# Two chained transformer blocks on one core: both blocks in one program section, weight slots and banks shared, with five reorderings

## The chip, the cores and the metric

The kernel runs on one core of a Trainium2 chip. The metric is the device time of one execution in microseconds (us), and the number compared is the median of several runs. TensorE (PE in the profile) multiplies, ScalarE (ACT) and VectorE (DVE) do the element-wise work, GpSimd (POOL) does small square roots and some transfers, and SyncE (SP) issues most transfers from main memory.

## The reference

A batch of one, 256 tokens, width 1024, all in float32. Two models run one after the other, two layers each.

```python
def reference(x, ...):
    x = first_block(x, c, positions, ...)    # per layer: adaLN scale/shift/gate from c, attention with rope and a
                                             # 31-tap conv branch, post-norm; MLP relu(u @ w_up)**2 @ w_down, post-norm:
                                             # x = layer_norm(ALPHA * x + (1 + gt2) * h, ln_ffn_g[l], ln_ffn_b[l])
    return second_block(x, rel_bias_table_2, ...)

def second_block(x, ...):
    for l in range(2):
        h = rmsnorm(x, ln_mix_g[l])
        proj = h @ w_in[l]                   # 1024 x 4128: q, k, v of branches A and B, latents of branch C
        ya = dilated_window_attention(...)   # with a bias looked up from rel_bias_table
        lam = exp(sum(lambda_q1 * lambda_k1)) - exp(sum(lambda_q2 * lambda_k2)) + lam_init
        yb = differential_attention(..., lam, bias_b)
        yc = mla_attention(...)
        x = x + (gates[0] * (ya @ w_br_a) + gates[1] * (yb @ w_br_b) + gates[2] * (yc @ w_br_c)) @ w_o[l]
        h = rmsnorm(x, ln_ffn_g[l])
        x = x + (silu(h @ w_ffn_gate[l]) * (h @ w_ffn_up[l])) @ w_ffn_down[l]
    return rmsnorm(x, final_norm_g)
```

## The kernel before

**Products.** Every large product is float32 split in two parts, a high and a low one. A weight group is 256 rows by up to 512 columns. It passes through a ring of four slots: SP loads it into `w_raw`, ACT rounds it into `w_hi` (line 123), DVE subtracts and leaves `w_lo` (line 129), and TensorE multiplies it with the transposed rows in twelve matmuls (lines 143 to 145: high by high, high by low, low by high, for two chunks and two token halves, tok 0 and 1). SP may load a slot again when its low part is made, and ACT may write `w_hi` again when TensorE has used it. A tile is the four groups that make one bank pair, `prod`; four more banks, `acc`, hold sums, and two, `turn`, take transposes. Rows are transposed on TensorE (line 203), ACT takes the high part (224) and DVE the low part (231).

**Order.** All is written out by hand for each engine, with semaphores between them. Each engine does its instructions in order, and so does SP, whose loads of weights thus stand in one queue with those of vectors.

**The end of a layer of the first block.** Its MLP has eight chunks f = 0 to 7. For each, DVE squares the hidden rows (line 1079), makes four low parts, adds one chunk of the second gate (`gate2_chunk`, line 1059, 128x1024), and makes the low parts of the transposed hidden rows. After the last chunk TensorE sums the gate over the partitions (`sum_rows`, line 1158) and then does the last down product: 48 matmuls into `acc`, tok 0 first. ACT copies the gate out of the bank (629). DVE then adds the residual for each of four half rows (lines 1008, 1012 and 764, `last_residual`), POOL makes the root, and the rows are normed. Between the two layers of the first block the next layer's input is normed first, half by half, with the norm's scale and the modulation folded together in `ada_first` (lines 1112 to 1115), and `x_res` itself (773 and 775, 128x1024) afterwards. At the end of the last layer only `x_res` is made.

**The change of blocks.** The first block ends its program section: all five engines meet at a barrier, and its memory and banks are given back. The second block's section begins with transfers that need its own memory: the flip matrix and the rope table (1539, 1540) and a 1.5 MB transfer from scratch on POOL (1614). TensorE reverses the bias rows with the flip matrix in six banks (12 products of 128x256, line 2199), DVE and ACT copy them out (1526, 1527), and only then does DVE set the semaphores that let SP load the first weights (116) and the norm's vector `mix_g` (1552). After the four groups of the first tile SP issues ten vector transfers (1554 to 1561), the last two being the gate's bias, 1.5 MB, and `ffn_g`, 0.5 MB. The second block's input product has 12 tiles of 344 columns; tiles 0 to 3 hold the latents. DVE waits for all ten vectors, makes the products for lambda (1928 to 1931), and then the low parts of tile 1.

**The end.** After the last down product DVE adds the residual (1861), ACT squares (1673), POOL makes the root (1619 to 1633), DVE multiplies by root and gain at once (1856, 128x1024 for each token half). Another section holds the one transfer of the whole 1 MB output (2438).

## Time and profile before

| what | value |
|---|---|
| median of three runs | 1939.33 us (1937.77 to 1939.8) |
| the profiled execution, its own time | 1941.2 us |
| its span, first to last instruction | 1939.4 us |
| TensorE busy | 1808.5 us, 93% of the span |
| VectorE busy | 1306.2 us, 67% |
| ScalarE busy | 870.9 us, 45% |
| mean granted TensorE clock | 0.976 of full speed |

TensorE is busy nearly all the time, so the table says that time can only be won where TensorE waits or runs at the lower clock. The stretches where it does so are found in the 40 slices of the page, and then in the timeline.

### The profile page before, as it was taken

What the parts mean: (1) busy time and instruction counts of PE and PEld (TensorE: products, weight loads), DVE (VectorE), ACT (ScalarE), POOL (GpSimd) and SP (SyncE); (2) the same over time, 40 slices, a digit from 0 to 9 for tenths busy, and PEclk for the clock granted to TensorE, in tenths of its full rate; (3) what the DMA queues carried; (4) which work ended last, traced back from release to release, by engine and by line L of the source; (5) the groups of instructions that cost most, each with busy time, mean ns of one, the idle gap of its engine ahead of it and who ended that gap; (6) DMA issues with size and microseconds to landing.
All of it is one profiled execution on the core that took longest, in us unless ns stands there. A gap on an engine that the chain in (4) does not pass through costs nothing.

```text
span 1939.4 us, 26122 instructions
## 1 busy us (share of the span) xinstructions
PE 1808.5 (93%) x8358; PEld 1423.0 (73%) x8358; DVE 1306.2 (67%) x2015; ACT 870.9 (45%) x1458; POOL 53.8 (3%) x116
## 2 busy tenths in 40 slices
PE   7989989998989999996699999999999999999997
PEld 3755767886755678884699767788879976778886
DVE  4679886666779886555454788655555478865554
ACT  1434433443334434442355565444445566644443
POOL 0000000000000000000000000000000000000000
PEclk9999999999999999998799999999999999999999
DMA  8755567773755546652566433455565553355653
GB/s 291 250 159 169 182 206 246 243 248 104 260 160 172 174 162 233 202 195 69 187 184 191 147 104 120 152 185 184 178 207 181 178 163 123 102 160 176 195 176 117
DMA packets 210879, 345.90 MB, mean 178 GB/s; under 512 B 20105, under 2 KB 95799, under 8 KB 210533
## 3 DMA queue, kind: packets, MB, share of 16 engines
q1 hardware_dynamic: 208758, 337.79, 53.8%
q0 software_dynamic: 2032, 6.97, 1.1%
q8 instruction: 50, 0.82, 0.2%
q14 instruction: 39, 0.32, 0.1%
HBM read 343.62 MB, written 1.07 MB: 178 GB/s over the span
## 4 chain that ended last, share of the span: by engine, by line
issue 52%; POOLq 1%; POOL 0%; DVE 0%
POOLq L1631 0%; POOLq L1620 0%; POOLq L1629 0%; POOL x_rstd L1632 0%; DVE x_res L1856 0%; POOL gates L1614 0%; POOL x_rstd L1633 0%; POOL sub_rstd L1621 0%; POOL x_squares L1628 0%; POOLq L1639 0%; POOLq L1454 0%; POOL lat_rstd L1621 0%; POOLq L377 0%
## 5 line engine op out<-in xcount | busy, mean ns | idle before, releaser
L129 DVE TENSOR_TENSOR w_lo_b<-w_raw_b,w_hi_b 128x1024 fp32r<-128x1024 f32 (+3 forms) x336 | 362.2, 1100 | 189.5 <-ACT w_hi_b L123 187.9
L123 ACT CAST w_hi_b<-w_raw_b 128x1024 fp32r<-128x1024 f32 (+3 forms) x336 | 313.4, 951 | 167.2 <-PE prod_b L145 79.6
L129 DVE TENSOR_TENSOR w_lo_a<-w_raw_a,w_hi_a 128x1024 fp32r<-128x1024 f32 x232 | 280.6, 1222 | 136.5 <-ACT w_hi_a L123 133.8
L143 PE MATMUL prod_b<-w_hi_b,hT_hi 128*128 128x512 f32 (+1 forms) x912 | 342.7, 376 | 14.3 <-ACT proj_b L1661 8.2
L123 ACT CAST w_hi_a<-w_raw_a 128x1024 fp32r<-128x1024 f32 x232 | 240.9, 1049 | 234.2 <-PE acc_a L145 115.1
L145 PE MATMUL prod_b<-w_hi_b,hT_lo 128*128 128x512 f32 (+1 forms) x912 | 334.6, 367 | 0.0
L144 PE MATMUL prod_b<-w_lo_b,hT_hi 128*128 128x512 f32 (+1 forms) x912 | 333.5, 366 | 0.0
L143 PE MATMUL prod_a<-w_hi_a,uT_hi 128*128 128x512 f32 x592 | 244.8, 413 | 18.3 <-DVE w_lo_a L129 9.4
L145 PE MATMUL prod_a<-w_hi_a,uT_lo 128*128 128x512 f32 x592 | 237.6, 401 | 0.0
L144 PE MATMUL prod_a<-w_lo_a,uT_hi 128*128 128x512 f32 x592 | 237.5, 401 | 0.0
L143 PEld LDWEIGHTS prod_b<-w_hi_b,hT_hi 128*128 128x128 f32 x912 | 173.1, 190 | 45.7 <-DVE w_lo_b L129 13.0
L145 PEld LDWEIGHTS prod_b<-w_hi_b,hT_lo 128*128 128x128 f32 x912 | 173.1, 190 | 24.1
L144 PEld LDWEIGHTS prod_b<-w_lo_b,hT_hi 128*128 128x128 f32 x912 | 173.5, 190 | 21.1
L143 PEld LDWEIGHTS prod_a<-w_hi_a,uT_hi 128*128 128x128 f32 x592 | 113.4, 191 | 57.9 <-issue 17.2
L145 PEld LDWEIGHTS prod_a<-w_hi_a,uT_lo 128*128 128x128 f32 x592 | 113.4, 192 | 27.9
L144 PEld LDWEIGHTS prod_a<-w_lo_a,uT_hi 128*128 128x128 f32 x592 | 113.7, 192 | 24.4
L143 PE MATMUL acc_a<-w_hi_a,aT_hi 128*128 128x512 f32 x272 | 111.8, 411 | 4.5 <-DVE w_lo_a L129 4.5
L916 DVE SCALAR_TENSOR_TENSOR conv_acc<-hpad,conv_wT,conv_acc 128x256 f32<-128x256 f32 x232 | 102.5, 482 | 10.5 <-issue 1.3
L144 PE MATMUL acc_a<-w_lo_a,aT_hi 128*128 128x512 f32 x272 | 109.3, 402 | 0.0
L145 PE MATMUL acc_a<-w_hi_a,aT_lo 128*128 128x512 f32 x272 | 108.8, 400 | 0.0
L143 PEld LDWEIGHTS acc_a<-w_hi_a,aT_hi 128*128 128x128 f32 x272 | 52.3, 192 | 18.7 <-issue 6.2
L1232 PE MATMUL acc_a<-ada_raw,c_wide 128*128 128x512 f32 x128 | 62.4, 633 | 0.0
(320 smaller groups left out, 2446.5 us busy)
## 6 DMA issues: line engine op xcount, KB each, us to landing
w_raw_a<-in_w_in_dram SPq DMA_DIRECT2D x72, 512.0 KB, 4.2
w_raw_b<-in_w_in_dram SPq DMA_DIRECT2D x192, 172.0 KB, 2.4
w_raw_a<-in_w_up_dram SPq DMA_DIRECT2D x64, 512.0 KB, 4.7
w_raw_a<-in_w_down_dram SPq DMA_DIRECT2D x64, 512.0 KB, 4.5
ada_raw<-in_w_ada_dram SPq DMA_DIRECT2D x52, 512.0 KB, 6.6
w_raw_b<-in_w_gate_dram SPq DMA_DIRECT2D x96, 256.0 KB, 3.1
w_raw_b<-in_w_ffn_gate_dram SPq DMA_DIRECT2D x88, 256.0 KB, 3.5
w_raw_b<-in_w_ffn_up_dram SPq DMA_DIRECT2D x88, 256.0 KB, 4.2
```

Source lines behind the costliest of these rows:

```text
L123: act.copy(self.hi[:, s, 0:cols], self.raw[:, s, 0:cols]).then_inc(self.hi_done, 1)
L129: dve.tensor_tensor(self.lo[:, s, 0:cols], self.raw[:, s, 0:cols], self.hi[:, s, 0:cols].bitcast(F32), ALU.subtract).then_inc(self.lo_done, 1)
L143: pe.matmul(out, a_hi, w_hi, start=first and c == 0, stop=False)
L144: pe.matmul(out, a_hi, w_lo, start=False, stop=False)
L145: mm = pe.matmul(out, a_lo, w_hi, start=False, stop=last and c == chunks - 1)
L916: dve.scalar_tensor_tensor(out, rows, w, out, ALU.mult, ALU.add)
L1232: mm = pe.matmul(acc[0][:, :], c_wide[:, 2 * i + k, :], ada_raw[:, i, k * NT:(k + 1) * NT], start=i + k == 0, stop=False)
```

## The change

1. Both blocks are written into one section: `first_block` and `second_block` return one function for each engine, which run one after the other. The weight ring, its semaphores, `prod`, `acc`, `turn` and their semaphores are made once; the second block counts on from `GROUPS1`, `TILES1`, `TURNS1` and `SPLITS1`.
2. The second block's first eight weight groups are loaded right behind the first block's last. `mix_g` is loaded in the middle of the first block's last layer. The second block's first input is normed straight from the first block's statistics (`first_h`, with `ada_first` = the last norm's vectors times `mix_g`), low parts of weights between, and `x_res` itself (`last_x`) after it.
3. What needs the first block's memory to be free (flip, rope table, six small vectors, the 1.5 MB bias transfer) waits on `first_left`, which DVE sets behind `last_x`. Tiles 1, 2 and 3 go to the `acc` pairs and back to `prod`; the bias rows are reversed behind tile 3 (four banks) and tile 4 (two banks).
4. The gate's bias and `ffn_g` are loaded behind all groups of `w_in`, in both layers of the second block.
5. The low parts of tiles 1 to 3 come before the lambda products, in both layers.
6. The gate chunk of f = 7 comes before its four low parts, in both layers of the first block.
7. At the end root and gain are split: DVE multiplies by the gain early, POOL does fewer steps, DVE scales the left half rows and ACT the right, and four transfers of 256 KB leave from SP and ACT.

```diff
@@ class Weights @@
-        sp.wait_ge(self.lo_done, pos.count(1))
+        sp.wait_ge(self.lo_done, pos.count(1 + self.groups))
@@ first_block, sync, last layer's MLP @@
+                else:
+                    sp.dma_start(mix_g[:, :], dr["ln_mix_g_2"][0:1, :].to_broadcast([P, D])).then_inc(mix_in, 16)
@@ first_block, vector, hidden() @@
+                    if f == T_FF - 1:
+                        gate2_chunk(f)
                     if after:
                         split(after)
...
-                    gate2_chunk(f)
+                    if f < T_FF - 1:
+                        gate2_chunk(f)
@@ first_block, vector, end @@
+                else:
+                    dve.wait_ge(mix_in, 16)
+                    for v in range(2):
+                        dve.tensor_tensor(ada_first[:, v, :], ln_vec[:, 1 - v, :], mix_g[:, :], ALU.mult)
+                    dve.drain()
...
+            def first_h(tok, h):
+                cols = slice(h * NT, (h + 1) * NT)
+                if h == 0:
+                    dve.wait_ge(ln_rstd, layer(LAYERS - 1, TOKS + tok, 2 * TOKS).count(1))
+                normed(u_rows[:, tok, cols], x_res[:, tok, cols], tok, ada_first[:, 1, cols], ada_first[:, 0, cols]).then_inc(u_ready, 1)
@@ second_block, sync @@
-            sp.dma_start(flip, dr["flip"]).then_inc(consts_in, 16)
-            sp.dma_start(trig[:, :, :], dr["trig_2"].rearrange("(t p) e -> p t e", p=P)).then_inc(consts_in, 16)
...
-                in_tile(IN2_T - LAT_TILES, layer(l, 0, G2))
+                for t in range(2):
+                    in_tile(IN2_T - LAT_TILES + t, layer(l, 4 * t, G2))
+                if l == 0:
+                    sp.wait_ge(first_left, 1)
+                    sp.dma_start(flip, dr["flip"]).then_inc(consts_in, 16)
+                    sp.dma_start(trig[:, :, :], dr["trig_2"].rearrange("(t p) e -> p t e", p=P)).then_inc(consts_in, 16)
...
-                sp.dma_start(gates[:, 0, :], row("b_gate", 3 * D)).then_inc(vec_in, 16)
-                sp.dma_start(ffn_g[:, :], row("ln_ffn_g", D)).then_inc(vec_in, 16)
-                with sp.Fori(1, LAT_TILES) as t:
+                with sp.Fori(2, LAT_TILES) as t:
                     in_tile(t + (IN2_T - LAT_TILES), Pos(0, (l, G2), (t, 4)))
                 with sp.Fori(0, IN2_T - LAT_TILES) as t:
                     in_tile(t, Pos(4 * LAT_TILES, (l, G2), (t, 4)))
+                sp.dma_start(gates[:, 0, :], row("b_gate", 3 * D)).then_inc(late_in, 16)
+                sp.dma_start(ffn_g[:, :], row("ln_ffn_g", D)).then_inc(late_in, 16)
@@ second_block, scalar @@
+                if l == 0:
+                    split(layer(l, 0, G2), 4, KG * IN2_W)
+                    for n in range(4):
+                        take_h_hi(n)
+                    split(layer(l, 4, G2), 4, KG * IN2_W)
...
                 for tok in range(TOKS):
                     square_x(2 * l, tok)
+                if l == 0:
+                    split(layer(l, 8, G2), 4, KG * IN2_W)
@@ second_block, vector @@
+                if l == 0:
+                    last_residual(0, 0)
+                    last_residual(0, 1)
+                    split(layer(l, 0, G2), 1, KG * IN2_W)
+                    last_residual(1, 0)
+                    first_h(0, 0)
+                    first_h(0, 1)
+                    take_h_lo(0)
+                    last_residual(1, 1)
+                    split(layer(l, 1, G2), 2, KG * IN2_W)
...
+                    for tok in range(TOKS):
+                        split(layer(l, 4 + 2 * tok, G2), 2, KG * IN2_W)
+                        last_x(tok).then_inc(x_halves, 2)
+                    dve.drain().then_inc(first_left, 1)
@@ second_block, the end @@
+            for tok in range(TOKS):
+                act.wait_ge(x_gained, 2 * tok + 2)
+                act.wait_ge(x_rstd_done, 2 * TOKS * LAYERS + tok + 1)
+                act.activation(x_res[:, tok, NT:D], h_rows[:, tok, NT:D], ACT.Copy, scale=x_rstd[:, 0, tok:tok + 1])\
+                   .then_inc(scaled, 1)
+                act.wait_ge(scaled, tok + 1)
+                act.dma_start(out[0, tok * P:(tok + 1) * P, NT:D], x_res[:, tok, NT:D]).then_inc(out_done, 16)
```

Three places show how the rows move. The first is DVE's order at the last MLP chunk of the first block's second layer (names as in the code; `w_lo` is the low part of a weight group). Before:

```order
L1079 TENSOR_TENSOR proj<-proj 128x512 [waits prod_free0_a]
L1079 TENSOR_TENSOR proj<-proj 128x512 [waits prod_free1_a]
L129 TENSOR_TENSOR w_lo_a<-w_raw_a,w_hi_a 128x1024 [waits w_hi_done_a] x4
L1059 SCALAR_TENSOR_TENSOR proj<-proj,c_act 128x1024 [waits gate2_in1]
L231 SCALAR_TENSOR_TENSOR aT_lo<-turn_a,aT_hi 128x4x128 [waits turn_hi_a] x2
L1008 SCALAR_TENSOR_TENSOR proj<-ada_rest,acc_a 128x512 [waits down0_done,ada_taken,vec_in]
```

And in the changed kernel:

```order
L1080 TENSOR_TENSOR proj<-proj 128x512 [waits prod_free0]
L1080 TENSOR_TENSOR proj<-proj 128x512 [waits prod_free1]
L1060 SCALAR_TENSOR_TENSOR proj<-proj,c_act 128x1024 [waits gate2_in1]
L134 TENSOR_TENSOR w_lo<-w_raw,w_hi 128x1024 [waits w_hi_done] x4
L241 SCALAR_TENSOR_TENSOR aT_lo<-turn,aT_hi 128x4x128 [waits turn_hi] x2
L1124 TENSOR_TENSOR ada_first<-ln_vec,mix_g 128x1024 [waits mix_g_in,vec_in]
L1124 TENSOR_TENSOR ada_first<-ln_vec,mix_g 128x1024
L1009 SCALAR_TENSOR_TENSOR proj<-ada_rest,acc 128x512 [waits ada_taken,down0_done,mix_g_in]
```

The gate chunk has moved ahead of the four low parts, and two multiplications by `mix_g` stand ahead of the first residual.

The second is SP's queue around the change of blocks. Before:

```order
L116 DMA w_raw_a<-in_w_down_dram 128x2x512 [waits w_lo_done_a] x8
L1531 UNCONDITIONAL_BRANCH [waits barrier_Pool_Activation_PE_DVE_SP_release]
L1539 DMA proj_b<-in_flip_dram 128x128
L1540 DMA trig_b<-in_trig_dram 128x2x32
L1552 DMA mix_g<-in_ln_mix_g_dram 128x1024 [waits vec_free]
L116 DMA w_raw_b<-in_w_in_dram 128x344 [waits w_lo_done_b]
L116 DMA w_raw_b<-in_w_in_dram 128x344
...
L1554 DMA lat_g<-in_mla_q_norm_g_dram 128x768
...
L1560 DMA gates<-in_b_gate_dram 128x3072
L1561 DMA ffn_g<-in_ln_ffn_g_dram 128x1024
```

And in the changed kernel, where eight loads of `w_in`, not four, stand ahead of the wait:

```order
L121 DMA w_raw<-in_w_down_dram 128x2x512 [waits w_lo_done] x8
L121 DMA w_raw<-in_w_in_dram 128x344 [waits w_lo_done]
L121 DMA w_raw<-in_w_in_dram 128x344
...
L1573 DMA proj_b<-in_flip_dram 128x128 [waits first_left]
L1574 DMA trig_b<-in_trig_dram 128x2x32
L1575 DMA lat_g<-in_mla_q_norm_g_dram 128x768
L1576 DMA lat_g<-in_mla_kv_norm_g_dram 128x256
L1578 DMA lam_vec<-in_lambda_q_2_dram 128x64 x2
L1578 DMA lam_vec<-in_lambda_k_2_dram 128x64 x2
L1579 DMA lam_const<-in_lam_const_dram 128x2
L1580 DMA sub_g<-in_diff_subln_g_dram 128x128
```

The barrier and the wait for the bias are gone from ahead of the weights. Tile 2's weights (the ninth group and on) now stand behind `first_left` and the eight small transfers, and `b_gate` and `ffn_g` have gone down the queue, to just ahead of the first group of `w_uq`.

The third is TensorE's order at the same change. Before:

```order
L2157 UNCONDITIONAL_BRANCH [waits barrier_Pool_Activation_PE_DVE_SP_release]
L2199 MATMUL prod_b<-gates,proj_b 128x256 [waits bias_in,consts_in_b]
L2199 MATMUL prod_b<-gates,proj_b 128x256 x3
L2199 MATMUL acc_b<-gates,proj_b 128x256 x8
L203 MATMUL turn_b<-ident,proj_b 128x128 [waits turn_free0_b,h_ready_b]
```

In the changed kernel the reversal comes behind tile 3 and tile 4 (between the two pieces stand the 48 matmuls of tile 4):

```order
L2286 MATMUL acc<-gates,proj_b 128x256 [waits prod_free0,prod_free1,bias_in,consts_in_b]
L2286 MATMUL acc<-gates,proj_b 128x256 x7
L148 MATMUL prod<-w_hi,hT_hi 128x344 [waits w_lo_done,prod_free0]
...
L2286 MATMUL acc<-gates,proj_b 128x256 [waits bias_out]
L2286 MATMUL acc<-gates,proj_b 128x256
```

Four tiles of the second block thus run before TensorE needs anything that was loaded after the first block had left its memory, except tile 2's and 3's weights.

## Rows read from the trace of the kernel before

**Rows 1.** The page's 40 slices: TensorE's granted clock, in tenths of full speed.

```profile
PEclk9999999999999999998799999999999999999999
```

**Rows 2.** A stretch: busy us (records) by engine, then clock, DMA share, GB/s.

```profile
910.00:930.00 20.00, 6.35 (x23) 5.40 (x24) 6.61 (x9) 1.72 (x4) 3.17 (x3) 0.58 0.27 84
```

**Rows 3.** TensorE's timeline, change of blocks: start, us, op, tiles, idle before and releaser.

```profile
891.88 3.15 PE L1158 MATMUL prod_a<-proj,ones 128*128 128x512 f32 x4 [3.06 <-DVE proj L1059]
894.04 1.42 PE L143 MATMUL acc_a<-w_hi_a,aT_hi 128*128 128x512 f32 x1
...
906.36 0.40 PE L145 MATMUL acc_a<-w_hi_a,aT_lo 128*128 128x512 f32 x1
923.65 3.46 PE L2199 MATMUL prod_b<-gates,proj_b 128*128 128x256 f32 x8 [16.90 <-DMA gates<-bias_rows_dram]
926.95 3.62 PE L2199 MATMUL acc_b<-gates,proj_b 128*128 128x256 f32 x16
...
940.38 0.63 PE L143 MATMUL prod_b<-w_hi_b,hT_hi 128*128 128x344 f32 x1 [1.43 <-DVE w_lo_b L129]
...
957.08 0.65 PE L143 MATMUL prod_b<-w_hi_b,hT_hi 128*128 128x344 f32 x1 [6.45 <-ACT proj_b L1661]
...
989.58 0.35 PE L143 MATMUL prod_b<-w_hi_b,hT_hi 128*128 128x344 f32 x1
```

**Rows 4.** DVE's timeline at the first block's last gate chunk.

```profile
890.54 1.28 DVE L1059 SCALAR_TENSOR_TENSOR proj<-proj,c_act 128x1024 f32<-128x1024 f32 x1
891.74 1.28 DVE L231 SCALAR_TENSOR_TENSOR aT_lo<-turn_a,aT_hi 128x512 fp32r<-128x512 f32 x2
```

**Rows 5.** TensorE's timeline between the first block's two layers.

```profile
455.49 1.88 PE L1158 MATMUL prod_a<-ada_first,ones 128*128 128x512 f32 x4
...
461.93 3.28 PE L1158 MATMUL prod_a<-proj,ones 128*128 128x512 f32 x4 [3.69 <-DVE proj L1059]
464.23 1.41 PE L143 MATMUL acc_a<-w_hi_a,aT_hi 128*128 128x512 f32 x1
...
480.88 0.76 PE L143 MATMUL prod_a<-w_hi_a,uT_hi 128*128 128x512 f32 x1 [1.52 <-issue]
```

**Rows 6.** DVE's timeline: `x_res` normed between the layers, and later three low parts.

```profile
493.79 1.29 DVE L773 SCALAR_TENSOR_TENSOR x_res<-x_res,mv,ln_vec 128x1024 f32<-128x1024 f32 x1
...
954.71 2.71 DVE L129 TENSOR_TENSOR w_lo_b<-w_raw_b,w_hi_b 128x688 fp32r<-128x688 f32 x3 [0.97 <-ACT w_hi_b L123]
```

**Rows 7.** The page's transfers: issuer, count, KB each, median us to landing.

```profile
w_raw_b<-in_w_in_dram SPq DMA_DIRECT2D x192, 172.0 KB, 2.4
...
gates<-in_b_gate_dram SPq DMA_DIRECT2D x2, 1536.0 KB, 9.2
...
ffn_g<-in_ln_ffn_g_dram SPq DMA_DIRECT2D x2, 512.0 KB, 11.1
out_dram<-x_res SPq DMA_DIRECT2D x1, 1024.0 KB, 4.0
...
sub_g<-in_diff_subln_g_dram SPq DMA_DIRECT2D x2, 64.0 KB, 6.5
```

**Rows 8.** Transfers issued from 942 to 943 us (behind `b_gate` and `ffn_g`).

```profile
w_raw_b<-in_w_in_dram SPq DMA_DIRECT2D x1, 172.0 KB, 9.7
```

**Rows 9.** SP's queue: one vector's issue, and the first group of `w_uq`.

```profile
940.43 0.43 SPq L1559 DMA_DIRECT2D sub_g<-in_diff_subln_g_dram  x1
...
1031.91 11.35 SPq L116 DMA_DIRECT2D w_raw_b<-in_w_uq_dram  x12
```

**Rows 10.** ACT's and TensorE's timelines at that group: its rounding, its first matmul.

```profile
1038.70 0.84 ACT L123 CAST w_hi_b<-w_raw_b 128x768 fp32r<-128x768 f32 x1 [0.54 <-PE prod_b L145]
...
1045.07 0.42 PE L143 MATMUL prod_b<-w_hi_b,yaT_hi 128*128 128x384 f32 x1
```

**Rows 11.** DVE's and SP's timelines at the end of the program.

```profile
1933.45 1.28 DVE L1856 SCALAR_TENSOR_TENSOR x_res<-x_res,x_rstd,mix_g 128x1024 f32<-128x1024 f32 x1 [1.59 <-POOL x_rstd L1633]
...
1934.99 0.40 SPq L2438 DMA_DIRECT2D out_dram<-x_res  x1
```

395 lines of the change are left out of this document (237 added, 158 removed).

## The prediction

> **What bounds the kernel now.** I read the page first. TensorE is busy for 1808.5 of 1939.4 us, so an edit is worth what it takes out of TensorE's waits or out of its time at the lower clock. The 40 slices of the granted clock are full except at the 19th and 20th [rows 1], the change from the first block to the second. So I read that stretch in windows: from 910 to 930 us TensorE is busy for 6.35 of 20 us at a granted clock of 0.58, and the transfer engines have a share of 0.27 [rows 2]. Nothing is the bound there; it is a chain of waits. TensorE's timeline gives it link by link [rows 3]: the first block's last matmul starts at 906.36 and ends at 906.76; TensorE then waits 16.90 us for the bias transfer and reverses the bias until 930.6; the first matmul of tile 0 comes at 940.38, because the weights and `mix_g` are asked for only then; tile 1 comes at 957.08 after another 6.45 us, behind the ten vector transfers. Tile 5, from which both kernels do the same work in the same order, starts at 989.58. That start is my marker.
>
> The same view shows a smaller wait at the end of each layer of the first block: TensorE idles 3.06 us [rows 3] and 3.69 us [rows 5] for the gate chunk, and the matmul that follows the sum takes 1.42 and 1.41 us where later ones take 0.40 [rows 3, 5]: the clock has dropped to its lower level, 1.2 GHz.
>
> **The gate chunk first (two layers).** DVE makes the chunk at 890.54, right behind its four low parts, and the low parts of the hidden rows at 891.74, until 893.02 [rows 4]. With the chunk moved ahead, 1.20 us leave this place: the hidden low parts are done at 891.8. The gate sum no longer waits; unthrottled it takes 1.88 us [rows 5], and started 3.06 us earlier, at 888.8, it is over at 890.7. So the low parts are the next to be late, and the down product starts at about 892.0 instead of 894.04 [rows 3]: 2.0 us. The moved chunk delays one low part of weights by 1.2 us; what hides that is the ring of four groups ahead of TensorE, whose 48 matmuls take 12.7 us (894.04 to 906.76 [rows 3]). The idle time falls from 3.06 to some 1.3 us, which may or may not keep the clock up. The 1.42 us matmul and the slow ones behind it are worth up to 1.3 us; I take 0.8, for between 0 and 1.3. So **2.8 us** in each layer, bounds 2.0 and 3.3. The first layer's is a term of its own; the second's goes into the next.
>
> **The change of blocks.** The model for the new sequence is in the trace: between the first block's two layers DVE does the same residuals, norm and low parts in the same order. There the down product starts at 464.23 and the next layer's first matmul at 480.88 [rows 5]: 16.65 us, less the same 0.8 of clock, 15.9. From 892.0 that puts tile 0 at 907.9 instead of 940.38. The two extra multiplications by `mix_g`, 128x1024 like those of 1.28 us [rows 4], take 2.6 us and lie beside the first quarter of the down product, some 3 of its 12.7 us; without that cover they would cost 2.6.
>
> From the first matmul at 480.88 to DVE's first instruction on `x_res` at 493.79 are 12.9 us [rows 5, 6], which ends the low parts of the input: 920.8. Now DVE makes four low parts of tile 1, of 0.9 us [rows 6], and norms `x_res`, four instructions of 1.29 us [rows 6]: 8.7 us. `first_left` comes at 929.5. TensorE runs out of work at the same time: tile 1 starts near 921 and takes about 8.
>
> Then SP stands where it stood not before: it issues ten small transfers ahead of tile 2's weights, 0.43 us each and a gap [rows 9], 4.5 in all, so these are issued at 934.0. When they land is not shown. Such a load takes 2.4 us in an undisturbed queue [rows 7] and 9.7 behind all ten vectors of before [rows 8]. Of those, 2 MB are gone from ahead of it, but the bias transfer of 1.5 MB on POOL starts at the same time, and the small vectors are slow themselves (`sub_g`, 64 KB, takes 6.5 [rows 7]). I take 6.0, nearer to the middle, which gives 940.0. Rounding and low part, 0.8 and 0.9 us, bring TensorE to 941.7: **a new wait of 12 us**, with the lower clock behind it.
>
> Tiles 1 to 4 took from 957.08 to 989.58, 32.5 us, with the same slow start [rows 3]. Three tiles take 24.8 (three quarters, and the whole of the slow start). The reversal is the same work, 16 records in 3.62 us at full clock [rows 3], so 5.4 for 24. Its inputs have long landed by 958, and its copies lie beside tile 4. Tile 5 starts at 941.7 + 24.8 + 5.4 = 971.9, against 989.58: **17.7 us** earlier. Bounds from the landing: 2.4 gives 21.3; 9.7 gives 14.0.
>
> In the second block's second layer the lambda products waited for nothing that TensorE missed, so their move is worth nothing there; in the first layer it is in the sum above.
>
> **The late vectors (two layers).** `b_gate` and `ffn_g` now stand ahead of the first group of `w_uq`, which was issued at 1031.91 [rows 9], rounded at 1038.70 and multiplied at 1045.07 [rows 10]. So there are 13.2 us from issue to use. `ffn_g` lands 11.1 us after its issue [rows 7], and the group behind it some 1 us later, near 1044; rounding, the latents' high and low parts that ACT and DVE do behind it, and the low part take 2 to 4 us. That is 1 to 3 us late, with a slow start up to 5. But the 11.1 was measured with six vectors ahead; alone, the two may land in 8, which hides them. Bounds 0 and 5 us for each layer; I take 1, nearer to the hidden end: **+2.0 us**.
>
> **The end.** The last multiplication waits 1.59 us for POOL, takes 1.28 us and ends at 1934.73; the transfer is issued at 1934.99 and lands 4.0 us later [rows 7, 11]. POOL has two steps to do instead of five behind the last square: about 0.9 of the 1.59. A half row takes half of 1.28: 0.6. The last pair is 512 KB instead of 1 MB; between 2.4 us for 172 KB and 4.0 for 1 MB [rows 7] I take 3.4: 0.6. Together **2.1 us**, bounds 0.9 and 3.5. The Trainium skill, "DMA: Bandwidth & Descriptors", section "Rules for kernel authors", speaks against the four transfers: transfers of two halves serialize, and queues of several engines share the same 16 transfer engines, so the split adds no bandwidth. By that rule the term loses its last 0.6 and the time is 0.6 us longer; no row here has a store of half the size to decide it.
>
> **Sum.** 2.8 + 17.7 − 2.0 + 2.1 = 20.6 us off a span of 1939.4: 1918.8. The profiled execution's own time (1941.2) lies 1.8 above its span, and the median (1939.33) is where the span is; I apply the difference to the median: **1918.7 us**.
>
> **Rivals.**
> (a) *Tile 2's weights come much later.* For it: the 9.7 us row [rows 8], and POOL's 1.5 MB at the same time. 9.7 us and 3 more for sharing put tile 5 at 978.6; the time is 1925.4. Against it: the 2 MB ahead are gone. The same page of the Trainium skill, section "Queues, rings and completion order", says that a transfer engine goes round between the queues that have work, packet by packet; by that rule POOL's transfer and SP's share from 930 on, as in this rival. Chance 0.2; it lies in my range.
> (b) *The late vectors are exposed*, 4 to 5 us in each layer: 1925 to 1929 with the rest as forecast, up to 1935 together with (a). For it: 11.1 us. Against it: 13.2 us of room. Chance beyond the range 0.1.
> (c) *No change:* what comes off at the change of blocks comes back at the first group of `w_uq`. It needs 10 to 13 us in each layer. 1936 to 1943, 0.04.
> (d) *Slower:* the late vectors hold up not one group of `w_uq` but all six, since each load waits for a low part that waits for the one before, and TensorE restarts slowly twice: 11.1 us and 4 more in each layer, 30 in all, against 22.6 gained: 1946.8. It decides from 11.3 us a layer. The 13.2 us of room speak against it. 0.04.
> (e) *More gain:* weights at 2.4 us, clock kept, vectors hidden: 3.6 + 1 + 2 + 1.4 less, 1911; beyond 1909, 0.06.
>
> **How the numbers follow.** The forecast, with (a), (b) and (e) as far as they stay between 1909 and 1929, has 0.76. From 1929 to 1935 there are 0.1. A measurement of this kernel tells 0.2%, 3.9 us, from no change. Faster is 0.76 + 0.1 + 0.06, or 0.92; same 0.04; slower 0.04.
>
> **What would show it.** The gate sum ahead of the last down product without a wait, and that product's first matmul under 1.4 us. Tile 0 at about 905 (908 less the first layer's 2.8). A wait of about 12 us ahead of tile 2, ended by ACT's rounding, which waited for `w_raw`. The reversal behind tile 3 with no wait of its own. At the first group of `w_uq` a TensorE wait of 0 to 3 us. I am wrong if tile 2's wait is under 8 or over 16 us, or if ACT waits for `w_uq` for more than 5 us.

## The result, and the profile after

The changed kernel takes **1921.3 us** (median of four runs, 1917.55 to 1923.12), beside 1939.57 us for the kernel before on the same chip: a ratio of 0.9903, 95% interval 0.9891 to 0.9915. The forecast was 1918.7, range 1909 to 1929. The profiled execution has a span of 1921.2 us, 18.2 less than before.

The page of the changed kernel, its line of the granted clock. The low slices, 8 and 7 in [rows 1], are 8 and 8.

```profile
PEclk9999999999999999998899999999999999999999
```

TensorE's timeline of the changed kernel, both ends of the first block's layers and the change of blocks (start, us, op, tiles, idle before and releaser); it answers to [rows 3, 5].

```profile
454.83 1.88 PE L1170 MATMUL prod<-ada_first,ones 128*128 128x512 f32 x4
...
461.33 0.47 PE L148 MATMUL acc<-w_hi,aT_hi 128*128 128x512 f32 x1 [1.40 <-DVE aT_lo L241]
...
476.86 0.77 PE L148 MATMUL prod<-w_hi,uT_hi 128*128 128x512 f32 x1 [1.52 <-issue]
...
884.42 1.88 PE L1170 MATMUL prod<-proj,ones 128*128 128x512 f32 x4
887.69 0.47 PE L148 MATMUL acc<-w_hi,aT_hi 128*128 128x512 f32 x1 [1.40 <-DVE aT_lo L241]
...
898.77 0.40 PE L150 MATMUL acc<-w_hi,aT_lo 128*128 128x512 f32 x1
900.51 0.65 PE L213 MATMUL turn<-ident,proj 128*128 128x128 f32 x4 [1.34 <-DVE proj L776]
902.64 0.63 PE L148 MATMUL prod<-w_hi,hT_hi 128*128 128x344 f32 x1 [1.48 <-issue]
...
940.66 0.65 PE L148 MATMUL acc<-w_hi,hT_hi 128*128 128x344 f32 x1 [15.20 <-DVE w_lo L134]
...
958.44 3.61 PE L2286 MATMUL acc<-gates,proj_b 128*128 128x256 f32 x16
...
971.00 0.51 PE L148 MATMUL prod<-w_hi,hT_hi 128*128 128x344 f32 x1
...
1028.19 0.42 PE L148 MATMUL prod<-w_hi,yaT_hi 128*128 128x384 f32 x1 [1.45 <-DVE ybT_lo L241]
```

The gate sum of the second layer has no wait and the down product behind it starts at a short 0.47 us. Tile 0 of the second block starts at 902.64 instead of 940.38, 3.5 us behind the first block's last matmul. Then stands the new wait, 15.20 us ahead of tile 2, and the marker, tile 5, at 971.00 instead of 989.58. The wait is opened in the queues of SP, POOL and ACT.

```profile
924.42 0.33 SPq L1573 DMA_DIRECT2D proj_b<-in_flip_dram  x1
...
929.57 0.44 SPq L1580 DMA_DIRECT2D sub_g<-in_diff_subln_g_dram  x1
930.37 82.60 SPq L121 DMA_DIRECT2D w_raw<-in_w_in_dram  x80
```

```profile
924.69 1.09 POOL L1639 DMA_DIRECT2D gates<-bias_rows_dram  x1 [17.45 <-DVEq L1984]
925.80 0.20 POOL L1653 TENSOR_TENSOR x_squares<-x_sq 128x1 f32<-128x1 f32 x1
935.56 0.19 POOL L1644 TENSOR_TENSOR x_squares<-x_squares,small 128x1 f32<-128x1 f32 x1 [9.56 <-issue]
```

```profile
938.93 1.62 ACT L128 CAST w_hi<-w_raw 128x688 fp32r<-128x688 f32 x2 [13.22 <-DMA w_raw<-in_w_in_dram]
```

`first_left` comes at 924.4, the ten small transfers (flip, rope table and the eight of the vectors) take 5.95 us of SP, tile 2's first group is issued at 930.37 and rounded at 938.93, 8.56 us later. Of POOL's root one instruction runs behind the transfer and the next starts 9.56 us later; the last section shows what it waits for.

At the end (ACT's timeline, and the view of the transfers: count, KB each, median us to landing), for [rows 7, 11]:

```profile
1917.53 0.72 ACT L1902 ACTIVATE x_res<-proj_b,x_rstd 128x512 f32<-128x512 f32 x1 [0.64 <-POOL x_rstd L1676]
1918.28 0.34 ACTq L1905 DMA_DIRECT2D out_dram<-x_res  x1
```

```profile
out_dram<-x_res SPq DMA_DIRECT2D x2, 256.0 KB, 2.1
out_dram<-x_res ACTq DMA_DIRECT2D x2, 256.0 KB, 2.6
```

The start of TensorE's last matmul, the mark for the end's term, in the kernel before and in the changed one:

```profile
1929.25 0.40 PE L145 MATMUL acc_b<-w_hi_b,yaT_lo 128*128 128x512 f32 x1
```

```profile
1914.36 0.40 PE L150 MATMUL acc<-w_hi,yaT_lo 128*128 128x512 f32 x1
```

**The ledger** is the difference of start times between the two traces at the same work. Before anything that differs it is −0.66 already (454.83 for 455.49), scatter between two executions. At the second layer's first matmul it is −4.02, at tile 5 −18.58, at the first group of `w_uq` −16.88 (1028.19 for 1045.07), at the last matmul of the program −14.89 (1914.36 for 1929.25), at the end of the span −18.2. The loss of 2.0 us between `w_uq` and the last matmul belongs to this one trace: the second trace of the changed kernel (e11) gains 1.0 there (1029.06 and 1912.22 at the same two places).

### The profile page after: what moved, and what is told of

Read it like the earlier page. It is cut to its first block, busy times and chain, and to the rows that moved or that the text cites. A ratio compares the mean times of both kernels' runs of the same rounds, so it can differ in the third digit from the quotient of the medians.

```text
span 1921.2 us, 26005 instructions
## 1 busy us (share of the span) xinstructions
PE 1807.1 (94%) x8358; PEld 1423.2 (74%) x8358; DVE 1310.8 (68%) x2025; ACT 871.5 (45%) x1460; POOL 53.0 (3%) x112
## 4 chain that ended last, share of the span: by engine, by line
issue 52%; PE 30%; DVE 10%; DVEq 4%; ACT 1%; POOLq 1%; DMA 1%; SPq 1%; POOL 0%; ACTq 0%
PE prod L148 5%; PE prod L150 5%; PE prod L149 5%; PE acc L148 4%; PE acc L150 4%; PE acc L149 4%; DVE w_lo L134 3%; DVE conv_acc L917 2%; DVEq L916 2%; PE acc L1244 2%; PE turn L213 1%; DMA ada_rest<-in_w_ada_dram 1%; DVEq L775 1%; DVE stats L765 0%; DVE x_res L1013 0%
## 5 line engine op out<-in xcount | busy, mean ns | idle before, releaser
L134 DVE TENSOR_TENSOR w_lo<-w_raw,w_hi 128x1024 fp32r<-128x1024 f32 (+3 forms) x568 | 642.1, 1150 | 339.1 <-ACT w_hi L128 334.5
L128 ACT CAST w_hi<-w_raw 128x1024 fp32r<-128x1024 f32 (+3 forms) x568 | 554.2, 990 | 416.4 <-PE acc L150 197.0
L148 PE MATMUL prod<-w_hi,hT_hi 128*128 128x512 f32 (+1 forms) x880 | 332.2, 378 | 8.2 <-ACT kv_up L1687 1.8
L150 PE MATMUL prod<-w_hi,hT_lo 128*128 128x512 f32 (+1 forms) x880 | 323.9, 368 | 0.0
L149 PE MATMUL prod<-w_lo,hT_hi 128*128 128x512 f32 (+1 forms) x880 | 322.8, 367 | 0.0
L148 PE MATMUL prod<-w_hi,uT_hi 128*128 128x512 f32 x592 | 244.7, 413 | 17.1 <-DVE w_lo L134 8.0
L150 PE MATMUL prod<-w_hi,uT_lo 128*128 128x512 f32 x592 | 237.9, 402 | 0.0
L149 PE MATMUL prod<-w_lo,uT_hi 128*128 128x512 f32 x592 | 237.7, 402 | 0.0
L150 PEld LDWEIGHTS prod<-w_hi,hT_lo 128*128 128x128 f32 x880 | 166.6, 189 | 24.0
L149 PEld LDWEIGHTS prod<-w_lo,hT_hi 128*128 128x128 f32 x880 | 167.1, 190 | 21.2
L148 PE MATMUL acc<-w_hi,hT_hi 128*128 128x512 f32 (+1 forms) x144 | 57.2, 397 | 19.8 <-DVE w_lo L134 17.7
L149 PEld LDWEIGHTS acc<-w_lo,aT_hi 128*128 128x128 f32 x272 | 51.9, 191 | 12.7 <-issue 0.2
```

Of the source, the lines that this page charges most:

```text
L128: act.copy(self.hi[:, s, 0:cols], self.raw[:, s, 0:cols]).then_inc(self.hi_done, 1)
L134: dve.tensor_tensor(self.lo[:, s, 0:cols], self.raw[:, s, 0:cols], self.hi[:, s, 0:cols].bitcast(F32), ALU.subtract).then_inc(self.lo_done, 1)
L148: pe.matmul(out, a_hi, w_hi, start=first and c == 0, stop=False)
L149: pe.matmul(out, a_hi, w_lo, start=False, stop=False)
L150: mm = pe.matmul(out, a_lo, w_hi, start=False, stop=last and c == chunks - 1)
```

## The experiments

All times are medians; each run was timed beside the kernel before on the same chip. "The changed kernel" is 1921.3, and 1921.0 in a second run of it (e11).

**e1, the gate chunk back behind its low parts.**

```diff
-                    if f == T_FF - 1:
-                        gate2_chunk(f)
                     if after:
                         split(after)
...
-                    if f < T_FF - 1:
-                        gate2_chunk(f)
+                    gate2_chunk(f)
```

> The changed kernel with its sixth part undone: the gate chunk of f = 7 stands again behind its four low parts, in both layers of the first block. Theory T (the chunk's place is worth its start and the clock behind it): each layer loses 2.2 us of start of the last down product and 1.1 to 1.2 us of clock in that product, 3.4 us a layer as between the two traces, and nothing hides it, because the second layer's loss also moves first_left and so tile 2's weights: 1928.1 us, +6.8 on 1921.3, ratio to the kernel before 0.994. The first matmul of the down product takes 1.4 us again. Rival R1 (the second layer's part is covered by the wait of 15.20 us ahead of tile 2): 1924.7, +3.4. Rival R2 (only the clock is won, the start comes from elsewhere in the merged section): +2.4, 1923.7.

Measured: 1926.04 us, ratio 0.9930 (0.9916 to 0.9943): 4.7 to 5.0 us slower than the changed kernel, between T and R1. The trace shows T's two pieces, and something given back behind them that T missed. TensorE's timeline of e1:

```profile
480.95 0.77 PE L148 MATMUL prod<-w_hi,uT_hi 128*128 128x512 f32 x1 [1.52 <-issue]
...
910.32 0.63 PE L148 MATMUL prod<-w_hi,hT_hi 128*128 128x344 f32 x1 [1.48 <-issue]
...
947.14 0.65 PE L148 MATMUL acc<-w_hi,hT_hi 128*128 128x344 f32 x1 [15.11 <-DVE w_lo L134]
```

The first layer ends 4.1 us later and tile 0 starts 7.7 us later than in the changed kernel, of which 0.75 is scatter that stands ahead of anything that differs (455.58 for 454.83). So the two layers lose 3.3 and 3.6 us, as T said. But tile 2 starts only 6.5 us later. The difference is the clock in tile 0. In windows of 10 us from the start of tile 0 (busy us and records by engine, then granted clock, DMA share, GB/s), first of e1, then of the changed kernel:

```profile
910.32:920.32 10.00, 8.52 (x39) 6.72 (x40) 8.51 (x13) 1.20 (x2) 1.70 (x2) 0.86 0.36 108
```

```profile
902.64:912.64 10.00, 9.46 (x34) 8.74 (x35) 7.63 (x12) 1.20 (x2) 1.71 (x2) 0.52 0.35 108
```

So R1's reason, the wait ahead of tile 2 as a cover, is refuted: the wait is as long as ever (15.11 us), and the missing 1.2 us are tile 0's clock: `first_left` comes 20.65 us behind tile 0 here, and 21.8 in the changed kernel. Another 0.9 come back between tile 2 and the reversal, which take 16.84 us at a granted clock of 0.89 for 17.78 at 0.84. That leaves 4.8 at tile 5 (5.54 less the 0.75), the measured cost. Whether the chunk's place has a part in that clock stays open: it was 0.52 to 0.54 in eight traces with the chunk early, but 0.86 in e5's and full in e4's and e8's.

**e12, the same part alone in the kernel before** (the edit of e1 reversed, in the kernel before).

> The kernel before with the sixth part alone: the gate chunk of f = 7 ahead of its four low parts. It prices that part without the changed change of blocks. Theory T: 3.4 us in each layer (start 2.2, clock 1.1 to 1.2), and the second layer's is not hidden, because the barrier and everything behind it follow the last matmul: 1932.5 to 1933.5, -6.8 us. Rival R (as undoing it in the changed kernel cost only 4.7 to 5.2, a part is given back behind it in either kernel): -4.5 to -5.5 us, 1934 to 1935.

Measured: 1933.92 us, ratio 0.9968 (0.9956 to 0.9980): 6.0 us faster, and by the ratio 6.2, between 3.9 and 8.5. T (6.8) fits, R (5.5 at most) is not excluded. The trace has both: up to the reversal it is 6.6 us ahead of the kernel before (915.24 for 923.65, less 1.8 of scatter at the start), and then the reversal runs at a granted clock of 0.65 instead of 0.78 and tile 0 is only 4.7 ahead. Together with e1 the part is worth 5 to 6 us.

**e2, tile 2's loads ahead of `first_left`.**

```diff
-                for t in range(2):
+                for t in range(3 if l == 0 else 2):
                     in_tile(IN2_T - LAT_TILES + t, layer(l, 4 * t, G2))
...
-                with sp.Fori(2, LAT_TILES) as t:
+                with sp.Fori(3 if l == 0 else 2, LAT_TILES) as t:
```

> The four loads of tile 2's weights are issued ahead of the wait for first_left and the ten small transfers; all else as in the changed kernel. Theory T (the 15.20 us wait is SP's place in the queue: 1.6 us until first_left, 6.0 for the ten issues, 8.5 to landing): loads issued by 921.7, rounding by ACT right behind its squares at 925.8, tile 2 at 927.5 instead of 940.66. Tile 3's weights then stand behind the small transfers, and its bank pair behind the root that POOL finishes at 938.4: tile 3 at about 941 to 943 instead of 950.87, a wait of 3 to 6 us ahead of it, total 1912 to 1914, -8 us. Rival R1 (the wait only moves: tile 3 now waits for the landing as tile 2 did and the time stays within 2 us): 1919 to 1922. Rival R2 (the bias transfer comes late behind it and the reversal waits): tile 3 as in T but a wait ahead of the reversal, 1916 or more.

Measured: 1913.74 us, ratio 0.9869 (0.9854 to 0.9884), 7.4 us faster than the changed kernel, as T said. Its TensorE and ACT timelines:

```profile
926.72 0.43 PE L148 MATMUL acc<-w_hi,hT_hi 128*128 128x344 f32 x1 [1.87 <-DVE w_lo L134]
...
941.02 0.63 PE L148 MATMUL prod<-w_hi,hT_hi 128*128 128x344 f32 x1 [6.46 <-DVE w_lo L134]
```

```profile
938.33 0.99 ACT L1693 ACTIVATE proj_b<-prod,x_rstd 128x344 f32<-128x344 f32 x2 [10.57 <-POOL x_rstd L1658]
939.20 1.44 ACT L128 CAST w_hi<-w_raw 128x688 fp32r<-128x688 f32 x2
```

The wait of 15.20 us is now 1.87, and 6.46 us stand ahead of tile 3. Two things end within 1 us of each other there. ACT waits 10.57 us for POOL's root, and tile 3's rounding stands behind it in ACT's order. But tile 3's first group, issued behind the ten small transfers and beside POOL's transfer, has landed whole only at 938.99, 0.2 us ahead of its rounding, so its landing alone would have cost almost as much.

**e3, tile 2's loads behind `first_left` but ahead of the ten small transfers.**

```diff
                     sp.wait_ge(first_left, 1)
+                    in_tile(IN2_T - LAT_TILES + 2, layer(l, 8, G2))
                     sp.dma_start(flip, dr["flip"]).then_inc(consts_in, 16)
```

> Tile 2's four loads stay behind the wait for first_left but go ahead of the ten small transfers. It tells the landing from the issue. Theory T (ten issues cost 6.0 us, and the vectors' own packets most of the 8.5 us landing, since they stand ahead in the same queue): first load issued at 924.4, landed by 928 although POOL's 1.5 MB start at the same time, tile 2 at 930 instead of 940.66; tile 3 again waits for weights behind the vectors, at 943 to 945 instead of 950.87: 1914 to 1916, -6 us. Rival R1 (the bias transfer is what makes the landing slow): landing stays at 8 us, first load landed at 932.5, tile 2 at 934.3 and tile 3 at 946 to 950: 1917 to 1920, -1 to -4 us.

Measured: 1914.51 us, ratio 0.9865 (0.9850 to 0.9881), T's time, for half of T's reason. ACT's timeline of e3:

```profile
927.70 0.76 ACT L128 CAST w_hi<-w_raw 128x688 fp32r<-128x688 f32 x1 [1.62 <-DMA w_raw<-in_w_in_dram]
934.74 0.76 ACT L128 CAST w_hi<-w_raw 128x688 fp32r<-128x688 f32 x1 [6.28 <-DMA w_raw<-in_w_in_dram]
```

The view of the transfers of e3, issues from 924 to 925 us, and then from 926 to 927:

```profile
w_raw<-in_w_in_dram SPq DMA_DIRECT2D x1, 172.0 KB, 2.4
...
w_raw<-in_w_in_dram SPq DMA_DIRECT2D x3, 172.0 KB, 7.9
```

TensorE starts tile 2 at 929.43 and waits once more, 3.36 us, at 936.47. Only what is issued at once lands as fast as T wanted. What is issued from 926 on, beside POOL's 1.5 MB and ahead of all vectors, lands 7.9 us after its issue, as R1 said. The Trainium skill, "DMA: Bandwidth & Descriptors", section "Queues, rings and completion order", says that a transfer engine goes round between the queues that have work, a packet at a time; these rows agree, since nothing but weights stood ahead in SP's queue.

**e4, the bias transfer later** (POOL: roots first, then a wait for the twelfth rounded group, then the transfer).

```diff
+                if l == 0:
+                    pool.wait_ge(first_left, 1)
+                    pool.wait_ge(bias_rows.in_dram, 16)
+                    pool.wait_ge(W.hi_done, layer(0, 11, G2).count(1 + W.groups))
+                    pool.dma_start(bias_flipped, bass.AP(tensor=scratch.tensor, offset=0,
+                                                         ap=[[1, P], [REL, AH + BH], [1, SEQ]])).then_inc(bias_in, 16)
```

> POOL issues the bias transfer behind its first roots and only once the sixteenth-less-four, that is the twelfth, weight group is rounded, so it shares nothing with tile 2's weights; the ten small transfers stay ahead. Theory T (sharing: 1.5 MB of the 3 MB moved between 925 and 937 us are the bias, at some 300 GB/s 4 to 5 us): tile 2's first group lands 4 to 5 us after its issue instead of 8.5, tile 2 at 936.5 instead of 940.66, the bias lands by 951 ahead of its reversal: 1917 to 1918, -4 us. The roots, which POOL made only at 935.6 to 938.4, are made by 929. Rival R1 (the small vectors' many packets make the landing slow, the bias none of it): landing stays 8 us, 1921, no change. Rival R2 (the bias is late for its reversal): a wait of some us ahead of the reversal, 1921 or more.

Measured: 1916.66 us, ratio 0.9883 (0.9867 to 0.9899), 4.4 to 4.6 us faster, T's time. SP's, ACT's and TensorE's timelines of e4:

```profile
928.52 30.01 SPq L121 DMA_DIRECT2D w_raw<-in_w_in_dram  x32
```

```profile
934.86 1.63 ACT L128 CAST w_hi<-w_raw 128x688 fp32r<-128x688 f32 x2 [10.04 <-DMA w_raw<-in_w_in_dram]
```

```profile
936.59 0.66 PE L148 MATMUL acc<-w_hi,hT_hi 128*128 128x344 f32 x1 [12.00 <-DVE w_lo L134]
```

Without POOL's transfer beside them the ten issues take 4.99 us (923.53 to 928.52) instead of 5.95, and issue to rounding is 6.34 us instead of 8.56. Those are 3.2 us, all of the step from a wait of 15.20 to one of 12.00. In this run tile 0 also ran at full clock, which chance gave (last section): `first_left` comes 20.6 us behind tile 0 instead of 21.8. So 1.1 of the 4.1 us by which tile 2 starts earlier in this trace are not the edit's, and T's 936.5 was met partly by luck; the landing, 5.2 and 5.8 us for the two loads of the first group, was slower than T's 4 to 5.

**e5, both causes together, and tile 3's loads ahead of the eight vectors** (edits of e2 and e4; the transfer waits for the thirteenth group).

> Both causes of the wait ahead of tile 2 and of the one that e2 moved to tile 3 are taken away together: tile 2's loads ahead of first_left as in e2, tile 3's loads behind flip and rope table but ahead of the eight vectors, POOL's roots ahead of its bias transfer, and that transfer issued only when tile 3's first group is rounded. Theory T (SP's place in the queue and POOL's transfer are all that TensorE waits for here): tile 2 at 926.7 as in e2, tile 3 at 934 to 936 with a wait under 2 us, the reversal near 943, tile 5 at 955 to 957 instead of 971.00 (e2: 963.18): 1905 to 1908, -14 us on the changed kernel and -7 on e2. Rival R1 (the bias transfer, issued near 931 and landing 11 us later, is late for its reversal): a wait of 2 to 5 us ahead of the reversal, 1909 to 1911. Rival R2 (the vectors, now ahead of tile 4's weights and beside the bias transfer, make tile 4 wait as they did tile 3): 4 to 6 us back, 1911 to 1913.

Measured: 1910.13 us, ratio 0.9844 (0.9831 to 0.9858); T's 1905 to 1908 is missed. Both rivals' waits are there, each smaller than they said: 1.35 us ahead of the reversal, 2.13 ahead of tile 4. ACT's and TensorE's timelines of e5:

```profile
946.07 1.67 ACT L128 CAST w_hi<-w_raw 128x688 fp32r<-128x688 f32 x2 [7.89 <-DMA w_raw<-in_w_in_dram]
```

```profile
944.01 3.69 PE L2289 MATMUL acc<-gates,proj_b 128*128 128x256 f32 x16 [1.35 <-issue]
949.83 0.43 PE L148 MATMUL prod<-w_hi,hT_hi 128*128 128x344 f32 x1 [2.13 <-ACT proj_b L1696]
```

**e9, the eight vectors behind tile 4's loads, the bias transfer right behind the roots** (tile 2's loads ahead of `first_left`, as in e2).

```diff
                     sp.dma_start(trig[:, :, :], dr["trig_2"].rearrange("(t p) e -> p t e", p=P)).then_inc(consts_in, 16)
+                    in_tile(IN2_T - LAT_TILES + 3, layer(l, 12, G2))
+                    in_tile(0, layer(l, 16, G2))
```

> e5 gave 1910.1 with two small waits left: 1.35 us ahead of the reversal (bias issued 931.36, landed 12.6 later) and 2.13 us and a slow start ahead of tile 4, whose weights were issued at 937.55 behind the vectors and landed near 946. Here the eight vectors go behind tile 4's loads as well, and POOL issues the bias transfer right behind its roots, near 929, without waiting for a rounded group. Theory T (both waits come from these two places): no wait ahead of the reversal, tile 4 directly behind it at 946 to 947 instead of 949.83, tile 5 at 956 to 957 instead of 960.59: 1906 to 1907. Rival R1 (the bias transfer now shares with tile 3's weights and gives the time back ahead of tile 3): a wait of 2 us or more there, 1909 to 1911. Rival R2 (the vectors behind tile 4 delay tile 5's weights): the wait moves on to tile 5, 1909 or more.

Measured: 1905.74 us, ratio 0.9831 (0.9818 to 0.9845): T. TensorE's timeline of e9:

```profile
926.25 0.43 PE L148 MATMUL acc<-w_hi,hT_hi 128*128 128x344 f32 x1 [1.87 <-DVE w_lo L134]
...
938.84 0.43 PE L148 MATMUL prod<-w_hi,hT_hi 128*128 128x344 f32 x1 [0.96 <-DVE w_lo L134]
...
942.74 3.61 PE L2289 MATMUL acc<-gates,proj_b 128*128 128x256 f32 x16
```

Waits of 1.87 and 0.96 us are left of 15.20, and the reversal has none. R1's sharing is there in small: of tile 3's loads those issued up to 928.0 landed in 2.3 to 4.2 us, and the one issued at 928.50, behind POOL's transfer (927.76), in 8.6.

**e6, the late vectors in four pieces of 512 KB, one behind each of the last four tiles of `w_in`, in both layers.**

```diff
-                sp.dma_start(gates[:, 0, :], row("b_gate", 3 * D)).then_inc(late_in, 16)
-                sp.dma_start(ffn_g[:, :], row("ln_ffn_g", D)).then_inc(late_in, 16)
+                for t in range(4, IN2_T - LAT_TILES):
+                    in_tile(t, layer(l, 4 * LAT_TILES + 4 * t, G2))
+                    if t < 7:
+                        cols = slice((t - 4) * D, (t - 3) * D)
+                        sp.dma_start(gates[:, 0, cols], dr["b_gate_2"][ls, cols].to_broadcast([P, D])).then_inc(late_in, 16)
+                    else:
+                        sp.dma_start(ffn_g[:, :], row("ln_ffn_g", D)).then_inc(late_in, 16)
```

> The changed kernel with b_gate in three transfers of 512 KB and ffn_g as a fourth, one behind each of the last four tiles of w_in, in both layers, instead of 2 MB in one go ahead of w_uq. Theory T (the late vectors cost 1.5 to 2.5 us a layer at the first groups of w_uq, as the waits of 1.45 and 1.97 us and the shifts between the two traces say): those waits are gone, 1917 to 1919, -2 to -4 us. Rival R1 (the shift in the second layer is scatter from run to run, and the first's is all): -1.5 us, 1919.8. Rival R2 (the pieces hold up w_in's own groups): new waits in w_in's last tiles, 1921 or more.

Measured: 1918.35 us, ratio 0.9886 (0.9871 to 0.9901), 2.7 to 3.0 us faster, as T said; the interval doesn't exclude R1's 1919.8. The traces say that both layers have a part, the second a small one: from tile 5 to the last matmul e6 takes 938.2 us and e11, the changed kernel again, 940.3. From tile 5 to the first group of `w_uq` there are 57.19 us in the changed kernel (57.12 in e7 and e11), 55.64 in e6, and 55.49 before. The first matmuls of that group in e6's two layers have no wait, where the ten traces of the changed kernel and its variants with the vectors in one go have 0.56 to 1.97 us in the second layer:

```profile
1028.00 0.42 PE L148 MATMUL prod<-w_hi,yaT_hi 128*128 128x384 f32 x1
...
1519.90 0.42 PE L148 MATMUL prod<-w_hi,yaT_hi 128*128 128x384 f32 x1
```

**e7, one store of 1 MB from SP.**

```diff
+            sp.wait_ge(out_ready, TOKS)
+            sp.wait_ge(scaled, TOKS)
+            sp.dma_start(out.rearrange("a (t p) d -> p (a t) d", p=P), x_res[:, :, :]).then_inc(out_done, 16)
```

> The changed kernel, with one transfer of 1 MB from SP when all four half rows are scaled, instead of four of 256 KB from SP and ACT. It measures the last part of the end's term. Theory T (the rest of the end's gain is not in the stores): the last scaling ends where it did, 18.25 - 14.36 = 3.9 us behind TensorE's last matmul's start, and the store takes 4.0 us and 0.3 to issue instead of 2.6: the stretch from the last matmul's start to the end is 8.4 us instead of 6.84 and the time 1.6 us longer, 1922.9. Rival R1 (by the Trainium skill, DMA: Bandwidth & Descriptors, Rules for kernel authors, a split adds no bandwidth): the store costs the same either way and the stretch stays within 0.3 us of 6.84, 1921.3.

Measured: 1922.68 us, ratio 0.9915 (0.9901 to 0.9928); the interval alone doesn't decide, the trace does. ACT's last scaling, SP's store and its landing in e7:

```profile
1913.80 0.72 ACT L1902 ACTIVATE x_res<-proj_b,x_rstd 128x512 f32<-128x512 f32 x1 [0.64 <-POOL x_rstd L1676]
```

```profile
1914.60 0.40 SPq L1632 DMA_DIRECT2D out_dram<-x_res  x1
```

```profile
out_dram<-x_res SPq DMA_DIRECT2D x1, 1024.0 KB, 4.1
```

From the last matmul's start (1910.63) to the end of the span (1919.0) are 8.37 us, T's 8.4, against 6.84 (1914.36 to 1921.2) with four stores. The split is worth 1.5 us. The rule of the Trainium skill ("DMA: Bandwidth & Descriptors", section "Rules for kernel authors") that splitting adds no bandwidth is not contradicted: three quarters of the output leave before the last half row is scaled, and what remains on the path is a store of 256 KB that lands 2.6 us after its issue.

**e8, the lambda products ahead of the low parts again** (DVE's wait for the vectors and its four instructions stand ahead of the loop over the low parts).

> The changed kernel with its fifth part undone: DVE waits for the vectors and makes the lambda products ahead of the low parts of tile 2 and on in the first layer of the second block (of tile 1 and on in the second), not behind those of tile 4. Theory T (worth nothing where the weights land behind the vectors anyway): in the first layer four small instructions, 1 us at most, stand between the weights' landing and tile 2's low parts, and may lie inside the wait; in the second layer 0. 1921 to 1922.5. Rival R1 (the wait on the vectors was a part of the 6.45 us that the kernel before lost ahead of its tile 1): 3 us or more ahead of tile 2, 1924 or more.

Measured: 1927.75 us, ratio 0.9938 (0.9925 to 0.9952), 6.5 to 6.7 us slower. Neither theory: in the first layer it costs next to nothing (tile 2's wait is 15.54 us), in the second, where T said 0, all. DVE's and TensorE's timelines there, and the same matmul in the changed kernel:

```profile
1433.85 0.29 DVE L2000 TENSOR_TENSOR lam_prod<-lam_vec 128x128 f32<-128x128 f32 x1 [7.82 <-DMA sub_g<-in_diff_subln_g_dram]
```

```profile
1435.56 0.65 PE L148 MATMUL prod<-w_hi,hT_hi 128*128 128x344 f32 x1 [5.06 <-DVE w_lo L134]
```

```profile
1433.56 0.42 PE L148 MATMUL prod<-w_hi,hT_hi 128*128 128x344 f32 x1 [1.70 <-ACT proj_b L1693]
```

The wait ahead of tile 1 is 3.4 us longer than in the changed kernel, and the granted clock over the 10 us behind it is 0.77 instead of 1.00. The cause is the second part of the change: it loads tile 1's weights ahead of the vectors in the second layer too (`for t in range(2)` in the diff), and those loads wait for free slots. So the last small vector lands 14.6 us behind tile 0's first matmul here, where in the kernel before even `ffn_g`, the last of ten, landed 6.0 us behind it. The fifth part is what keeps DVE from waiting for them.

**e10, everything moved** (e9 and e6 together).

> e9 and e6 together: vectors behind tile 4, bias right behind the roots, b_gate and ffn_g in four pieces in w_in's last tiles. Theory T (the two gains lie in different places of the program and add): e9's time less 2.5 to 3 us, 1903 to 1904.5, ratio to the kernel before 0.981. Rival R (with the change of blocks shorter, SP's queue is fuller at w_in's last tiles and the pieces hold it up): e9's time less 1 us at most.

Measured: 1904.57 us, ratio 0.9816 (0.9803 to 0.9829), the best of all: some 35 us faster than the kernel before and 16.5 faster than the changed one. On e9 it gains 1.2 us by the medians, 2.9 by the ratios; the intervals overlap. The traces say more: from tile 5 to the last matmul e10 takes 938.3 us and e9 941.8, so the pieces gain 3.5 us there, as T said, and no wait is left at `w_uq`. But tile 5 itself starts at 957.66 instead of 955.30, behind waits of 1.48 us ahead of tile 3 and 0.90 ahead of tile 5. Those lie ahead of the first piece, in the part that is the same as e9's, so they are no sign of R; e9's trace has 0.96 and none.

**e11, the changed kernel again.**

> The changed kernel once more, unedited, to see what repeats of its trace. Expected: a median of 1920 to 1922.5. The wait ahead of tile 2 within 0.4 us of 15.2, as in e1, e6, e7 and e8 (15.1 to 15.5). At the first groups of w_uq in the second layer the stretch from its tile 1 to the first matmul with the latents' second half was 107.8 us in the changed kernel's first trace and 105.3 to 105.8 in e1, e2, e3, e5 and e7, which are the same there: if the 107.8 was scatter it is 105 to 106 here, if not it is 107.8 again.

Measured: 1921.02 us, ratio 0.9897 (0.9881 to 0.9912). The wait ahead of tile 2 is 15.12 us: it repeats. The second layer's stretch at `w_uq` does not. The windows from its first `w_uq` matmul to the first on the second half of the latents, first of the changed kernel's first trace, then of e11:

```profile
1522.18:1541.39 19.21, 17.54 (x89) 16.61 (x89) 8.36 (x11) 9.96 (x18) 0.00 (x0) 0.91 0.60 177
```

```profile
1521.56:1539.21 17.65, 15.97 (x88) 15.06 (x89) 8.36 (x11) 9.97 (x18) 0.00 (x0) 1.00 0.63 196
```

The wait ahead of it was 1.97 us in the first and 0.56 in e11, and the clock fell in the first alone (0.91 for 1.00): 1.56 us of the ledger are scatter, and 1.5 more between the two layers' `w_uq` groups. Counted from the first mark (455.49), e11 ends 21.0 us ahead of the kernel before, and the changed kernel's first trace 17.5; the medians of the two are only 0.3 us apart.

## Why the prediction was right, and by how much each step was off

**The gate chunk.** Forecast 2.8 us a layer. The first layer gives 4.02 − 0.66 = 3.4: the start 2.24 earlier (461.33 for 464.23, less the 0.66), the clock 1.12 (16.65 us from that matmul to the next layer's first became 15.53). The second layer's product starts at 887.69, or 891.7 on the time axis of the kernel before, forecast 892.0. Both layers together were forecast at 5.6 us; the ledger says 6.5 to 7, the medians of e1 and e12 say 5 to 6.

**Tile 0.** Forecast 907.9 without the first layer's shift, measured 902.64 + 4.02 = 906.7 on the same axis. The stretch between the layers was the right model; the chain was 14.95 us instead of 15.9.

**The wait ahead of tile 2.** Forecast 12 us, measured 15.20, within the 8 to 16 that I had set. It ended as said: DVE's low part came right behind ACT's rounding, which had waited 13.22 us for `w_raw`. `first_left` was right (21.8 us behind tile 0, 21.6 forecast), and so was rounding and low part (1.73 for 1.7). Two terms were mis-sized: the ten issues took 5.95 for 4.5 us, and issue to rounding, which I had marked as not shown, 8.56 for 6.0, together 4.0 too little. Tile 2 came 38.0 us behind tile 0 instead of 33.8. The wait grew less than that, because tiles 0 and 1 kept TensorE for 22.8 us and not 21.6, at the lower clock. e4 shows 3.2 of it to be POOL's transfer, 1.0 in the issues and 2.2 in the landing. Rival (a) named the sharing with POOL's transfer and sized it too high (12.7 for 8.56).

**Tile 2 to tile 5.** 30.3 us, forecast 30.2; the reversal had no wait, as said.

**The sum of the change of blocks.** 18.58 − 4.02 = 14.6 us, forecast 17.7, bounds 14.0 to 21.3. No run takes the first three parts of the change back one by one: that the 14.6 come from the barrier, the bias and the loads that no longer stand ahead of tile 0 is read from the two traces.

**The late vectors.** Forecast 1 us a layer. The first layer lost 1.7 (57.19 for 55.49 us), e6 gave back 1.55 of it, and in all 2.7 to 3.0 us for two layers by the medians: right mechanism, up to 1 us too little. ACT waited 4.2 and 4.6 us for `w_uq`, under the 5 that I had set. In the second layer the cost scatters (waits of 0.56 to 1.97 us in repeated traces).

**The lambda products.** "Worth nothing there", said of the second layer, failed. I compared with the kernel before, where the vectors stood ahead of tile 1's weights, and did not ask what the part is worth beside the second one. e8: without it 6.5 us are lost. The forecast of the whole was not hurt, since both parts are in the kernel; that was luck.

**The end.** Forecast 2.1 us, measured 10.15 − 6.84 = 3.3, near the upper bound of 3.5. e7 shows the store to be 1.5 of it, where I had 0.6 for a smaller last pair.

In sum the forecast took 20.6 us off the span and 18.2 came off. Short of the forecast are 3.1 at the change of blocks, 0.7 at the first layer's late vectors and 1.0 behind them (the ledger goes from −16.88 to −14.89, forecast 1 us; e11 shows this last one to be scatter); beyond it are 0.6 in the first layer, 1.2 at the end and 0.66 of scatter at the start. So 4.8 us of one sign stand against 2.5 of the other: the mechanisms were right, and that the total was nearer than its parts is partly luck. Two traces of the same kernel differ by 3.5 us in this ledger, so a difference of 1 us in a single entry behind tile 5 tells nothing.

## What to carry to other kernels

When a barrier between two stages is taken away, the next limit is the first transfer that still waits for memory to be given back: put every load that doesn't need that memory ahead of the wait in its queue (e2, 7.4 us), and the vectors that are read late behind the weights that are read next (with that and the later bias transfer, e9, 15.4 us, beside the 18.3 of the change itself). Issue a large transfer on an engine only behind that engine's own short work that others wait for, above all where a drain stands in that work (next section). A large vector in the middle of a stream of weights went better in pieces of one or two weight groups' size. And price each part of a change also with the other parts in place: a part that is worth nothing alone may be the cover of another.
